# Where the low halves of the weights are formed, and how far ahead

## The chip, the cores and the metric

One core of a Trainium2 chip runs the whole program. The metric is device time in microseconds (us), from one launch. Engines: TensorE (PE, with its weight loads PEld), VectorE (DVE), ScalarE (ACT), GpSimd (POOL) and SyncE (SP), which issues the loads.

## The reference

Two transformer blocks in float32, on 512 tokens of 1024 features. What matters here:

```python
# first block: h = rms_norm(x)
proj = h @ w_in                      # r, k, v, decay, rate, gate, memory query
def step(S, inp):                    # delta rule, 12 heads of 64
    sa = einsum(S, a_t)
    S = S * w_t + sa * b_t + v_t * k_t
    return S, einsum(S, r_t)
x = x + concat([mix, mem_out]) @ w_out
x = x + square(relu(rms_norm(x) @ w_ff1)) @ w_ff2
# second block: two attentions, each with its gate
y = sigmoid(g_a) * (o_a @ w_branch_a) + sigmoid(g_b) * (o_b @ w_branch_b)
x = x + y @ w_out
x = x + (silu(h @ w_gate) * (h @ w_up)) @ w_down
```

## The kernel before

**Products with weights.** Every large product is made of three matmuls per block of 128 x 128: high half of the weights by high half of the activations, low by high, high by low. `weight_block` (L1083) issues them. The weights come as 216 units of 128 x 1024 float32 (`unit_list`, L2593), loaded by SP (`load`, L2509). The ScalarE function `split` (L2081) waits for the load and for the last matmul of the unit that used the same buffers before, and copies `Wraw` to `Whi` at the lower precision (L2090). Then `Wlo = Wraw - Whi` is formed: by DVE (L1643) if the plan gave the unit the kind "wlo", by POOL (L2418) if it gave "wlo_pool". PE's first block of a tile waits for this subtraction. There are three sets of buffers in turn (`NW = 3`); units 3 and 29 have sets of their own. A load waits for the subtraction that last read its `Wraw`.

**The plan.** `make_plan` (L197) writes one list of steps by hand-made rules, and each engine runs its own steps of that list in this order; it never goes past a step that waits. The helper `unit` (L230) is called when a tile starts on a new unit `u` and first puts into the list the splits of all units up to `u + ahead - 1` (`splits`, L220), so that with `ahead` 2 the split of unit `u + 1` stands in front of tile `u`. The state `lo` says which engine gets the subtraction.

```python
    def unit(name):
        u = state["units"]
        state["units"] += 1
        splits(u + state["ahead"])
        return u
```

**Stages in order of time.** First projections; then the recurrence over six head pairs, where `blend` (L173) mixes the steps of one pair's block inverse (`inverse`, L514: scores "xm" and "sb", turned copies "na", then five levels of "t1", "xt" and "xu", the last one "yu") with the projections of the next pair (`ahead`, L488) and the state steps and the tail of the pair before (`states`, L542, `tail`, L558). A pair consumes three units (key, receptance, value), so it holds three splits. In the plan they stand as follows:

- slot A: behind the first level's "xu", a state step and the key tile's shift; next come "t1" and "xt" of level 2, a state step, the scan of the decays ("cum", DVE L1791), "xu", a state step, and the exponentials (ACT)
- slot B: behind the third level's "xu" and the next tile's shift; next come "t1" and "xt" of level 4, the group norm's root (reciprocal and the copy that widens it, DVE L1677 and L1680), "kk" and "xu"
- slot C: behind the value tile's shift, "xm" (DVE L1829) and the bonus (DVE L1812); next comes "sb", seven masked copies on DVE (L1829, L1855, into MT, Yi and BR), whose banks PE needs for "na"

DVE's part of "t1" is L1879 (T), of "xu" L1886 (Xi), of a state step L1915 (PD), of "yu" L1893. POOL has in the recurrence some small steps of its own, as the addition of the identity to Xi and Yi (L2479). In the last pair the first tiles of the output product take the filler's place; the splits of units 28 and 29 stand together between two state steps.

Then the first block's output product and feed-forward stage, the second block's projections, its two attentions with gate tiles and branch tiles between them (`weave`, L164), the joined branches (kind "both": 4 units "bb", each for two tiles of four blocks; `evict`, L1747: multiply by the gate, add the other branch (L1754), cast on ACT (L2171), subtract (L1756)), and the second output product and feed-forward stage.

`ahead` is 2 from the start of the recurrence (L611) to the end, apart from one tile. `lo` is "wlo_pool" in the recurrence (set L613, reset L636) and from the attentions to the end of the joined branches (set L716, reset L742): 17 units (13 to 29) and 24 units (117 to 140).

Of the kernel before, what the change touches and what calls it, by code (L numbers as in the profile page):

```python
# [25 lines left out]
NW = 3  # L26
# [34 lines left out]
class Plan:  # L61
# [9 lines left out]
    def step(self, kind, *key):  # L71
        self.steps.append((kind, *key))
        self.count(kind, *key)
# [55 lines left out]
def run(gen):  # L129
    for _ in gen:  # L130
        pass


def turns(*gens):
    gens = list(gens)
    while gens:
        for g in list(gens):
            try:
                yield next(g)
            except StopIteration:  # L140
                gens.remove(g)
# [50 lines left out]
def spaced(gen, took):  # L192
    for _ in gen:
        yield took


def make_plan(units):  # L197
# [9 lines left out]
    state = {"loads": 0, "splits": 0, "units": 0, "lo": "wlo", "ahead": 1, "held": None}  # L207
    pend = []

    def flush():  # L210
        now, pend[:] = pend[:], []
        for f in now:
            f()
# [222 lines left out]
    def mem_attention():  # L436

        def item(n):
            hp, j = divmod(n, 4)
            for i in range(2):  # L440
                M.take(("ms", n, i))
            step("ms", n)
            for i in range(2):
                M.give(("ms", n, i))
            yield 0.4
            step("mn", n)
            yield from rounds(SOFT_ROUNDS)
            bank("mt", n)
            yield 0.5
            if j == 0:  # L450
                M.take(("mpv", hp))
            step("mv", n)
            if j == 3:
                step("mpv", hp)
                step("mpv_lo", hp)
                M.give(("mpv", hp))
            yield 0.5
        yield from pipeline([item(n) for n in range(8)])
# [24 lines left out]
    def bonus(p):  # L483
        step("bo", p)
        ftmp.give(("sq", p))
        yield 1.0
# [55 lines left out]
    def states(p, room=0.2):  # L542

        two("uw", p)
        yield 1.0
        two("pd", p)
        yield 0.5
        two("phi", p)
        yield 0.6
        two("yo1", p)  # L550
        yield 0.6
        for ch in range(1, NC - 1):
            step("st", p, ch)
            yield room
        bank("yo2", p)
        yield 0.9

    def tail(p):  # L558
        step("gsq", p)
        yield 0  # L560
        bank("root", "t", p)
        yield 0.9
        yield 0
        bank("tn", p)
        yield 0.5
        yield 0
        bank("tg", p)
        yield 1.0
        step("tlo", p)
        count("Ulo", "mix", p)  # L570
        yield 0
# [38 lines left out]
    flush()  # L610
    state["ahead"] = NW - 1  # L611

    state["lo"] = "wlo_pool"  # L613
    mem_att = mem_attention()
    mix_order = (0, 1, 2, 3, 4, 6, 7, 5)
    for p in range(NP - 1):
# [7 lines left out]
    def beside():  # L624
        yield from turns(itertools.chain(bonus(NP - 1), states(NP - 2), tail(NP - 2)), mem_att)
        step("Xload")
        for i, g in enumerate(outs):

            state["ahead"] = (NW - 1, NW, NW - 1)[i]
            yield from spaced(itertools.islice(g, 7), 0.8)  # L630
        state["ahead"] = NW - 1

    filler = beside()
    blend(itertools.chain(inverse(NP - 1), states(NP - 1, 0.6), spaced(tail(NP - 1), 1)), filler, FILL_LAST)
    run(filler)
# [99 lines left out]
    flush()  # L735
    flush()

    for m in range(4):
        hold = []
        run(tile("both", (2 * m,), ("bb", m), "att", range(4, 8), hold=hold, last=False))  # L740
        run(tile("both", (2 * m + 1,), ("bb", m), "att", range(4, 8), j0=4, keep=hold[0]))
    state["lo"] = "wlo"  # L742
    for i in range(8):
        run(tile("res", ("gffn2", i), ("wo2", i), "y2", range(8)))
    ahead_of.append(norm(("n", "gffn2")))
# [57 lines left out]

def block_program(nc, xT, memT, wts, vecs, cst, w2a2, g2, biasA, biasB, xN, memN, out, units):
    plan = make_plan(units)
    N = lambda *key: plan.numbers[key]
    tiles = plan.tiles
# [1942 lines left out]
```

## Time and profile before

| | |
|---|---|
| three runs | 1519.39, 1523.72, 1524.26 us |
| median | 1523.72 us |
| profiled execution | 1518.95 us, its span 1517.2 us |
| busy in the span | PE 1462.2 (96%), PEld 1156.8 (76%), DVE 800.4 (53%), ACT 552.7 (36%), POOL 239.4 (16%) |
| mean granted TensorE clock | 0.997 of full speed |
| DMA | 130.89 MB, mean 86 GB/s |

The profile is one execution. Busy time is the sum of an engine's instructions; what matters for an engine in order is also where it stands still, and until what. In timeline rows the first number is the start in us from the span's start, the second the length, then engine, line, operation, output<-inputs, shapes and count; in square brackets the idle time before and what ended it.

### The profile page before, as it was taken

Reading aid. Unit: us, or ns where it says so; the run is one execution under the profiler, and the core shown is the slowest. Engines: PE = TensorE matmul, PEld = TensorE weight load, DVE = VectorE, ACT = ScalarE, POOL = GpSimd, SP = SyncE. Lnnn points to the kernel's source line nnn. Section 1 sums busy time; section 2 is a strip of 40 time slices with the busy share of each in tenths; the row PEclk is TensorE's granted clock in tenths of the full one; section 3 lists DMA queues with packets and bytes.
Section 4 is the critical chain, followed back from the end, with each engine's and each line's share of the span. In section 5 each row is a group of like instructions: output and inputs, shape, how many; then the busy total and the mean of one; then the engine's idle time right before and its main releaser. Section 6 shows DMA issues by size and latency. Waiting matters only on the chain.

```text
span 1517.2 us, 26650 instructions
## 1 busy us (share of the span) xinstructions
PE 1462.2 (96%) x11374; PEld 1156.8 (76%) x11374; DVE 800.4 (53%) x1261; ACT 552.7 (36%) x942; POOL 239.4 (16%) x166
## 2 busy tenths in 40 slices
PE   7999999979999999999999999999999999999999
PEld 6867777756788888888788766767777888888887
DVE  5655566664564444535644358577554443443343
ACT  7444434363422221312442256545333221222221
POOL 0233333201200000000110012222322210220120
PEclk9999999999999999999999999999999999999999
DMA  8311011011223232333233133311222333323223
GB/s 323 112 30 44 30 30 44 23 52 58 70 87 108 84 108 87 98 97 97 84 97 96 58 107 96 94 56 53 83 92 89 97 97 98 97 85 109 84 88 107
DMA packets 39334, 130.89 MB, mean 86 GB/s; under 512 B 4272, under 2 KB 5296, under 8 KB 39216
## 3 DMA queue, kind: packets, MB, share of 16 engines
q1 hardware_dynamic: 39216, 129.18, 26.9%
q8 instruction: 90, 1.47, 0.4%
q14 instruction: 28, 0.23, 0.0%
HBM read 127.07 MB, written 2.10 MB: 85 GB/s over the span
## 4 chain that ended last, share of the span: by engine, by line
PE 82%; DVE 8%; ACT 4%; issue 3%; POOL 0%; POOLq 0%; ACTq 0%; DVEq 0%
PE bank L1047 79%; PE bank L1447 1%; DVE Wlo L1643 1%; ACT Whi L2090 1%; DVE qa L1754 1%; DVE z L1680 0%; DVE Xi L1886 0%; DVE qa L1752 0%; ACT Hhi L2171 0%; PE bank L1161 0%; DVE X L1725 0%; ACT kbr L2337 0%; ACT slab L2306 0%; PE bank L1237 0%; ACT tmpb L2205 0%
## 5 line engine op out<-in xcount | busy, mean ns | idle before, releaser
L1047 PE MATMUL bank<-Hhi,Whi 128*128 128x512 f32 x912 | 375.8, 412 | 11.6 <-DVE Wlo L1643 8.4
L1047 PE MATMUL bank<-Hhi,Wlo 128*128 128x512 f32 x912 | 360.9, 396 | 0.0
L1047 PE MATMUL bank<-Hlo,Whi 128*128 128x512 f32 x912 | 357.6, 392 | 0.0
L1047 PE MATMUL bank<-Uhi,Whi 128*128 128x512 f32 x736 | 290.9, 395 | 8.1 <-POOL Wlo L2418 3.1
L1047 PE MATMUL bank<-Uhi,Wlo 128*128 128x512 f32 x736 | 287.2, 390 | 0.0
L1047 PE MATMUL bank<-Ulo,Whi 128*128 128x512 f32 x736 | 287.0, 390 | 0.0
L2090 ACT CAST Whi<-Wraw 128x1024 fp32r<-128x1024 f32 (+1 forms) x216 | 222.9, 1036 | 164.2 <-PE bank L1047 148.2
L1643 DVE TENSOR_TENSOR Wlo<-Wraw,Whi 128x1024 fp32r<-128x1024 f32 (+1 forms) x175 | 224.2, 1282 | 98.9 <-ACT Whi L2090 98.8
L1047 PEld LDWEIGHTS bank<-Hhi,Whi 128*128 128x128 f32 x912 | 171.5, 188 | 66.0 <-issue 12.3
L1047 PEld LDWEIGHTS bank<-Hlo,Whi 128*128 128x128 f32 x912 | 171.9, 188 | 42.1
L1047 PEld LDWEIGHTS bank<-Hhi,Wlo 128*128 128x128 f32 x912 | 172.0, 189 | 34.0 <-issue 1.2
L1047 PEld LDWEIGHTS bank<-Uhi,Whi 128*128 128x128 f32 x736 | 138.1, 188 | 45.2 <-DVE Wlo L1643 5.5
L1047 PEld LDWEIGHTS bank<-Ulo,Whi 128*128 128x128 f32 x736 | 138.3, 188 | 29.4
L1047 PEld LDWEIGHTS bank<-Uhi,Wlo 128*128 128x128 f32 x736 | 138.3, 188 | 27.8 <-issue 0.2
L2418 POOL TENSOR_TENSOR Wlo<-Wraw,Whi 128x1024 fp32r<-128x1024 f32 x41 | 99.8, 2433 | 367.1 <-ACT Whi L2090 366.4
L1725 DVE TENSOR_TENSOR X<-X,bank 128x512 f32<-128x512 f32 x72 | 49.5, 688 | 168.8 <-PE bank L1047 168.7
L2426 POOL TENSOR_TENSOR accb<-accb,tmpb 128x512 f32<-128x512 f32 x14 | 18.8, 1344 | 383.9 <-ACT tmpb L2205 383.9
L2165 ACT CAST Uhi<-tmpb 128x512 fp32r<-128x512 f32 x32 | 19.8, 619 | 148.0 <-DVE tmpb L1734 148.0
L2431 POOL TENSOR_TENSOR qa<-qa 128x512 f32<-128x512 f32 x22 | 28.5, 1295 | 198.9 <-ACT qa L2175 198.9
L2179 ACT CAST Hhi<-qa 128x512 fp32r<-128x512 f32 x22 | 13.7, 622 | 116.0 <-POOL qa L2436 116.0
L2347 ACT ACTIVATE sr<-sr,st 128x256 f32<-128x256 f32 (+1 forms) x64 | 33.7, 528 | 36.6 <-DVE st L2015 19.8
L1732 DVE SCALAR_TENSOR_TENSOR tmpb<-bank,RSb 128x512 f32<-128x512 f32 x32 | 22.1, 692 | 44.8 <-PE bank L1047 44.6
(292 smaller groups left out, 1571.8 us busy)
## 6 DMA issues: line engine op xcount, KB each, us to landing
Wraw<-in_wts SPq DMA_DIRECT2D x208, 512.0 KB, 3.5
bA<-in_biasA SPq DMA_DIRECT2D x12, 256.0 KB, 2.8
Wraw<-in_wts SPq DMA_DIRECT2D x8, 384.0 KB, 3.2
x<-in_xT SPq DMA_DIRECT2D x8, 256.0 KB, 4.4
x_rows<-in_xN SPq DMA_DIRECT2D x2, 1024.0 KB, 8.3
X<-in_xT SPq DMA_DIRECT2D x2, 1024.0 KB, 7.2
out<-X SPq DMA_DIRECT2D x8, 256.0 KB, 2.1
bB<-in_biasB SPq DMA_DIRECT2D x4, 384.0 KB, 3.1
```

The costliest lines, as they stand in the source:

```text
L1047: return e.matmul(o, lhsT, rhs, start=start, stop=stop, skip_group_check=True)
L1447: p = e.transpose(o, sr[n % 3][:, x:x + 128], c("ident"))
L1643: e.tensor_tensor(Wsp[k][1][:, 0:width], Wraw[k][:, 0:width], Wsp[k][0][:, 0:width].bitcast(F), ALU.subtract).then_inc(S["wlo"])
L1725: e.tensor_tensor(y, y, z, ALU.add).then_inc(S["evict"])
L1732: e.scalar_tensor_tensor(z[:], b[:], 0.0, RSb[:], ALU.max, ALU.mult).then_inc(S["evict"])
L1754: e.tensor_tensor(z[:], z[:], gates[i], ALU.add).then_inc(S["gated"])
L2090: e.copy(Wsp[k][0][:, 0:width], Wraw[k][:, 0:width]).then_inc(S["whi"])
L2165: e.copy(Uhi[:, x.key[1], :], tmp_of(("raw", t))[:]).then_inc(S["ffhi"])
L2347: p = e.activation(part, part, ACT.Exp, scale=1.0, bias=x[:, 2 + i:3 + i], accum_out=x[:, 4 + i:5 + i])
L2418: done(e.tensor_tensor(Wsp[k][1][:, 0:width], Wraw[k][:, 0:width], Wsp[k][0][:, 0:width].bitcast(F), ALU.subtract), "wlo_pool")
L2426: done(e.tensor_tensor(accb[:], accb[:], tmp_of(("sqr", *x.key))[:], ALU.add), "sq_add")
L2431: done(e.tensor_tensor(z[:], z[:], s[:], ALU.mult), "sig")
```

## The change

`lo` stays "wlo" (DVE) through the recurrence, `ahead` becomes 3 from the end of the recurrence on, where it was set back to 2, and `lo` goes back to "wlo" before the joined branches and not after them. Nothing else differs.

```diff
@@ -610,7 +610,6 @@
     flush()
     state["ahead"] = NW - 1
 
-    state["lo"] = "wlo_pool"
     mem_att = mem_attention()
     mix_order = (0, 1, 2, 3, 4, 6, 7, 5)
     for p in range(NP - 1):
@@ -628,7 +627,7 @@
 
             state["ahead"] = (NW - 1, NW, NW - 1)[i]
             yield from spaced(itertools.islice(g, 7), 0.8)
-        state["ahead"] = NW - 1
+        state["ahead"] = NW
 
     filler = beside()
     blend(itertools.chain(inverse(NP - 1), states(NP - 1, 0.6), spaced(tail(NP - 1), 1)), filler, FILL_LAST)
@@ -735,11 +734,11 @@
     flush()
     flush()
 
+    state["lo"] = "wlo"
     for m in range(4):
         hold = []
         run(tile("both", (2 * m,), ("bb", m), "att", range(4, 8), hold=hold, last=False))
         run(tile("both", (2 * m + 1,), ("bb", m), "att", range(4, 8), j0=4, keep=hold[0]))
-    state["lo"] = "wlo"
     for i in range(8):
         run(tile("res", ("gffn2", i), ("wo2", i), "y2", range(8)))
     ahead_of.append(norm(("n", "gffn2")))
```

## Rows read from the trace of the kernel before

**Rows 1.** The tile Wlo of the whole span: duration min/median/max in ns.
```profile
L1643 DVE TENSOR_TENSOR Wlo<-Wraw,Whi x175: 951/1226/1652, 6.7 to 1506.3; 128x1024 fp32r<-128x1024 f32 x167, 128x768 fp32r<-128x768 f32 x8
L2418 POOL TENSOR_TENSOR Wlo<-Wraw,Whi x41: 2347/2385/2932, 88.1 to 1099.9; 128x1024 fp32r<-128x1024 f32 x41
```

**Rows 2.** Busy time by stage: PE, PEld, DVE, ACT, POOL (x instructions), clock, DMA, GB/s.
```profile
85.00:385.00 300.00, 271.97 (x5655) 209.01 (x5652) 179.20 (x400) 127.33 (x270) 83.48 (x60) 0.99 0.13 39
1075.00:1110.00 35.00, 29.83 (x127) 23.30 (x127) 25.33 (x28) 11.23 (x16) 9.46 (x4) 1.00 0.25 77
```

**Rows 3.** Timeline of 179 to 184, slot A of one head pair.
```profile
179.62 0.76 DVE L1879 TENSOR_TENSOR T<-bank,C 128x256 f32<-128x256 f32 x2 [0.53 <-PE bank L1047]
179.81 1.03 ACT L2090 CAST Whi<-Wraw 128x1024 fp32r<-128x1024 f32 x1
180.48 1.21 DVE L1791 TENSOR_TENSOR_SCAN sg<-C,sg 128x512 f32<-128x512 f32 x1
180.93 2.93 POOL L2418 TENSOR_TENSOR Wlo<-Wraw,Whi 128x1024 fp32r<-128x1024 f32 x1 [2.38 <-ACT Whi L2090]
181.65 0.69 PE L1047 MATMUL bank<-T,Yi 64*64 64x64 f32 x32
183.09 0.27 DVE L1915 SCALAR_TENSOR_TENSOR PD<-bank,PC,PD 128x64 f32<-128x64 f32 x1
183.47 0.33 PE L1047 MATMUL bank<-PD,AR 64*64 64x64 f32 x4
```

**Rows 4.** Timelines of 185 to 199, slot B of the same pair.
```profile
185.96 0.43 DVE L1680 COPY ftmp<-st 128x512 f32<-128x512 f32 x1
192.87 1.03 ACT L2090 CAST Whi<-Wraw 128x1024 fp32r<-128x1024 f32 x1
194.57 0.69 PE L1047 MATMUL bank<-T,Yi 64*64 64x64 f32 x32
194.97 1.67 DVE L1680 COPY z<-st 128x512 f32<-128x512 f32 x1
197.22 0.74 DVE L1886 TENSOR_TENSOR Xi<-bank,Xi 128x256 f32<-128x256 f32 x2
198.02 0.69 PE L1047 MATMUL bank<-Xi,MT 64*64 64x64 f32 x32 [0.67 <-DVE Xi L1886]
```

**Rows 5.** Timeline of 207 to 212, slot C of the same pair.
```profile
207.72 0.68 DVE L1812 SCALAR_TENSOR_TENSOR bonus<-bank,slab 128x512 f32<-128x512 f32 x1
207.89 1.29 POOL L2479 TENSOR_TENSOR Xi<-Xi,C 128x512 f32<-128x512 f32 x1 [3.94 <-DVE Xi L1829]
211.03 0.69 PE L1047 MATMUL bank<-C,AR 64*64 64x64 f32 x32 [1.79 <-DVE BR L1829]
```

**Rows 6.** Timeline of 101 to 104: a DVE operation beside one of POOL.
```profile
101.64 1.29 POOL L2470 TENSOR_TENSOR ta<-ta,kn 128x512 f32<-128x512 f32 x1
101.92 1.55 DVE L1820 TENSOR_TENSOR AR<-kn,Pp 128x512 f32<-128x512 f32 x1
```

**Rows 7.** Timeline of 368, the chain of state steps in the last head pair.
```profile
368.00 0.28 DVE L1915 SCALAR_TENSOR_TENSOR PD<-bank,PC,PD 128x64 f32<-128x64 f32 x1 [0.87 <-PE bank L1047]
```

**Rows 8.** Timelines of four places late in the kernel.
```profile
741.02 0.19 PEld L1047 LDWEIGHTS bank<-Uhi,Whi 128*128 128x128 f32 x1 [0.55 <-DVE Wlo L1643]
897.61 0.19 PEld L1047 LDWEIGHTS bank<-Hhi,Whi 128*128 128x128 f32 x1 [1.91 <-POOL Wlo L2418]
1092.85 2.56 DVE L1754 TENSOR_TENSOR qa<-qa,tmpb 128x512 f32<-128x512 f32 x1
1094.92 0.50 PE L1047 MATMUL bank<-Uhi,Whi 128*128 128x512 f32 x1 [1.68 <-POOL Wlo L2418]
```

**Rows 9.** A stretch at the lower clock, and POOL's slot A of the next two pairs.
```profile
260.00:264.00 4.00, 4.00 (x37) 3.30 (x29) 0.00 (x0) 0.91 (x3) 1.57 (x2) 0.59 0.42 131
229.51 2.92 POOL L2418 TENSOR_TENSOR Wlo<-Wraw,Whi 128x1024 fp32r<-128x1024 f32 x1 [2.39 <-ACT Whi L2090]
279.70 2.92 POOL L2418 TENSOR_TENSOR Wlo<-Wraw,Whi 128x1024 fp32r<-128x1024 f32 x1 [2.40 <-ACT Whi L2090]
```

## The prediction

> All times are microseconds unless ns is said. "Wlo" is the subtraction that forms the low half of a weight unit, "cast" the one on ScalarE that forms its high half. Units carry numbers 0 to 215 in the order of their use.
>
> **What bounds the kernel.** I read the engine totals first: TensorE (PE) is busy 96% of the span, DVE 53%, ACT 36%, POOL 16%. So a change of the other engines can pay or cost only through stalls of PE. The stage table says where stalls are: in the recurrence, 85 to 385, PE stands for 28 of 300, and over the joined branches (kind "both") for 5.2 of 35 [rows 2]; in the feed-forward stages it hardly stands. The list of waits and the timelines then name the releaser of each stall. In the recurrence PE never waits for a POOL Wlo: it waits for DVE results of the recurrence. Late in the kernel it does wait for Wlo of both engines [rows 8].
>
> **Part 1: Wlo of the recurrence moves from POOL to DVE.** Counting through the planner, POOL has units 13 to 29 there: 17 of the 41 in [rows 1]. POOL takes 2.39 for one, DVE 1.23 [rows 1]. The sum 17 x 1.23 = 21 isn't the price; it depends on what stands behind the Wlo in DVE's fixed order. The plan puts one at each of three places of a head pair.
>
> Slot A (units 16, 19, 22, 25; the planner's order is shift, cast, Wlo, then T of level 2, a state step, the scan). The cast ends at 180.84, so DVE, which has run T at 179.62 meanwhile, would stand until 180.9, run Wlo to 182.1 and T to 182.9. PE starts its matmuls on T at 181.65 without a wait now [rows 3]: it would start at 182.9, 1.3 late. Behind T stand a state step (0.3) and the 1.21 scan, so the addition to Xi (0.75) and the next state step (0.28, now at 183.09) end near 185.4, and PE, which needs that at 183.47, is 2.0 late altogether [rows 3]. ACT's exponentials wait for the same scan and come 2.7 later, with ScalarE's square root and DVE's reciprocal behind them; PE reaches the product that needs them with a little room. Four times 2.0 is 8.0. The first pair (unit 13) has no state steps, there only T counts: 1.4. Bounds: 1.2 each if only the subtraction counts, 2.8 if the late square root shows too. I take **9.4** (6 to 14).
>
> Slot B (units 14, 17, 20, 23, 26). The cast ends at 193.90, Wlo would run to 195.2 and T to 195.95, where PE has started on it at 194.57: 1.4 late [rows 4]. But the copy into z took 1.67 because POOL's Wlo ran beside it; the same form takes 0.43 without POOL (185.96), so I give 1.25 back [rows 4]. With it the addition to Xi, which waits for PE too, starts where it does now (197.22), and of PE's present wait of 0.67 the delay is hidden [rows 4]. What is left is 1.4 - 0.67 = 0.75, five times less a little in the first pair, whose T of the last level is late already: **3.5** (2 to 7).
>
> Slot C (units 15, 18, 21, 24). The cast is early. Wlo would stand between the bonus, which ends at 208.40, and seven masks of scores for whose last one PE already waits 1.79 [rows 5]. So its 1.25 adds in full. It also meets POOL's addition to Xi, which runs from 207.89 to 209.18 [rows 5]. What that does is seen elsewhere: a DVE product of two SBUF tensors that began at 101.92 beside POOL's 1.29 took 1.55 instead of about 0.7 [rows 5, 6]. It ran its own length once POOL was done, so Wlo would start near 209.2: 0.75 more. Four times 2.0: **8.0** (5 to 8).
>
> By the Trainium skill, "SBUF — State Buffer", section "Who interferes with whom", a DVE instruction with two SBUF inputs and a GpSimd one that reads SBUF exclude each other for the whole instruction. This trace agrees: 1.55 in [rows 6], 2.56 in [rows 8]. The rule speaks for this change at B and in the joined branches, and against it at C.
>
> Units 27 to 29, in the last pair. Unit 27 stands before the addition to Yi, behind which PE's solve waits; it costs between nothing and 1.23, and as slots A and B say that the cast comes late, I take 1.0. Units 28 and 29 stand together inside the chain of state steps, where DVE idles 0.87 per step [rows 7]; their casts are early, 2 x 1.23 less that slack and a part of what DVE idles before: 1.2 (0.7 to 2.5). Together **2.2** (0.7 to 3.7).
>
> What POOL gains is worth nothing: its steps of the recurrence wait for ACT, PE or DVE, and the 2.9 of its Wlo in slot A is over before the exponentials are done in the new order.
>
> Sum of part 1: 9.4 + 3.5 + 8.0 + 2.2 = 23.1.
>
> **The clock.** In one of four equal slots C the TensorE clock fell: between 260 and 264 the granted share was 0.59, thus 1.2 GHz for most of it against 2.4 around [rows 9], after a stall like the 1.79 of [rows 5]. That pair took 279.70 - 229.51 = 50.19, the one before it 229.51 - 180.93 = 48.58 [rows 3, 9]: 1.6 for one fall. The stall at C would be near 3.8 now, so more of them should be followed by a fall. I take two more, **3.2** (0 to 10).
>
> **Part 2: look-ahead of three units.** From unit 29 on, each split stands one tile earlier. On ACT the cast of unit u+2 now waits for the last matmul of unit u-1, but it stands behind the eviction of that tile, which waits for the same; on DVE and on SP's queue (a load waits for the Wlo of three units before) the order is the same with the index shifted. So no wait is added except for one extra split at unit 29, behind which PE has a tile to run (24 matmuls, by 29.83 for 127 of them 5.6 [rows 2]). What goes are PE's waits for Wlo from unit 31 on: six before the second block's norm, the longer ones 0.55 of weight load [rows 8], of which part is hidden under the matmul before, 1.1 in all; 1.5 of the 1.91 at the start of the attention [rows 8]; an estimated 0.8 in small ones later. The wait for unit 30's Wlo stays, since its split stands where it stood. Sum: -3.4 (0 to -6).
>
> **Part 3: Wlo of the joined branches on DVE.** POOL's Wlo blocks a DVE addition there, 2.56 for about 0.7, and PE waits 1.68 for the Wlo itself [rows 8]. DVE wins 1.9 a unit and pays 1.23, and the Wlo is no longer urgent. But the chain of evictions on DVE (multiply, add, wait for ACT's cast, subtract, twice per unit) is longer than PE's 5.6 per unit, and PE has two banks: it stays a bit late. Of PE's 5.2 [rows 2] I take half back: **-2.7** (+1 to -5.2). POOL keeps 20 Wlo (units 118 to 137), all in the attention, at an unchanged price.
>
> **Sum.** 23.1 + 3.2 - 3.4 - 2.7 = +20.2 on the profiled execution's 1518.95 gives 1539.2. The runs shown are 1519.39, 1523.72 and 1524.26, so the profiled one lies 4.8 under their median, and by the median I would get 1543.9. I put the forecast between: **1541**.
>
> **Rivals.**
> 1. *Faster.* Each Wlo runs in an idle stretch of DVE, and PE's later waits swallow the delays. For it: DVE is busy only 179 of 300 [rows 2]. It decides if the casts end well before DVE comes to the Wlo. Then all that is left are parts 2 and 3, -6.1 and at most -11: 1513 to 1518. Against it: in slots A and B the cast ends 1.2 and 0.8 after DVE wanted to go on. Chance 0.10.
> 2. *No change.* A third of the slots cost, the others are covered: about +6 - 6, 1519 to 1524. Chance 0.08.
> 3. *The clock falls at every A and C.* About eight more falls of 1.6, thus +13 where I took 3: 1550 to 1556. Chance 0.18. The Trainium skill, "TensorE: Matmul & The Clock Gate", section "What's actually happening", says that the clock is throttled by default and activity releases it; by that, a longer stall asks for a fall, and one of four here agrees so far [rows 9].
> 4. *The look-ahead does nothing*, since the cast that it moves waits for a tile that ends later; or the freed DVE time in the joined branches is lost to the chain there. Then 6 less is won: 1545 to 1550. Chance 0.12.
>
> The forecast's own case, 1530 to 1546, has 0.52. The range, 1527 to 1555, leaves out the faster rivals and the tail above. What a measurement of this kernel can tell from no change is 0.3%, about 4.6. Faster 0.10, same 0.08, slower 0.82.
>
> **What would show it.** Right: DVE with 196 Wlo and POOL with 20; the period of a head pair up from 48.6 to about 53; PE waiting about 1.3 for T in slot A and 3 to 4 for BR in slot C; DVE's Wlo in slot C near 2.0 long; the copy to z at 0.43; from 400 on a stage that is 5 to 7 shorter, with no waits like those of [rows 8]. Wrong: a pair period under 50 (the covers hold), or PE's waits of part 2 still there (the look-ahead doesn't reach), or a clock of 1.2 GHz in most pairs (the third rival).

## The result, and the profile after

| | before | after |
|---|---|---|
| median (lowest to highest) | 1523.16 us (1519.39 to 1524.26), 4 runs | 1541.35 us (1539.76 to 1544.11), 4 runs |
| ratio after / before | | 1.0128, 95% interval 1.0115 to 1.0141 |
| profiled execution, span | 1518.95, 1517.2 us | 1544.11, 1542.3 us |
| mean granted TensorE clock | 0.997 | 0.989 |

The change makes the kernel 18.2 us slower by the medians (+1.2%; the ratio in the table, which is not simply that of the two medians, gives +1.28%, or 19.5 us). The two profiled executions lie 25.2 apart, since the one of before was the fastest of its runs and the one of after the slowest of its own. Offsets below are between these two, for the same DVE operation in both traces; they add up to 25, not to 18.

The engine totals of the page and two of its groups of instructions after the change, line by line with busy time, mean ns of one, and the idle time before with its releaser:

```profile
PE 1472.4 (95%) x11374; PEld 1167.0 (76%) x11374; DVE 814.6 (53%) x1282; ACT 553.3 (36%) x942; POOL 187.2 (12%) x145
L1642 DVE TENSOR_TENSOR Wlo<-Wraw,Whi 128x1024 fp32r<-128x1024 f32 (+1 forms) x196 | 252.8, 1291 | 139.7 <-ACT Whi L2089 139.6
L2417 POOL TENSOR_TENSOR Wlo<-Wraw,Whi 128x1024 fp32r<-128x1024 f32 x20 | 47.8, 2391 | 253.6 <-ACT Whi L2089 253.6
```

The instructions moved as the plan says: 196 on DVE and 20 on POOL, against 175 and 41 in [rows 1]. The totals say nothing of the 25 us: PE is busy 10 us longer (the same number of matmuls, more of them at the lower clock), DVE is at 53% as before. The offsets by stage do:

| up to (us in after's trace) | offset | step |
|---|---|---|
| 85, start of the recurrence | 0 within 0.9 | 0 |
| 398, its end | +29.4 | +29 |
| 770, end of the first feed-forward stage | +27.8 | -1.6 |
| 1104, start of the joined branches | +29.1 | +1.3 |
| 1141, their end | +26.9 | -2.1 |
| 1516, last feed-forward stage | +25.2 | -1.8 |

So all of the loss is in the recurrence, and the later stages give 4 back, less than the 7.2 by which the same stages are shorter with parts 2 and 3 alone (below). What makes PE stand in the recurrence, from the list of PE's waits over 85 to 405 (in total, times, longest):

```profile
PE bank L1046 <- DVE BR L1828: 14.8, 5, 3.7
PE bank L1046 <- DVE T L1878: 7.8, 6, 2.5
PE bank L1160 <- DVE T L1878: 5.4, 4, 1.4
```

and the same list of the kernel before, over 85 to 385:

```profile
PE bank L1047 <- DVE BR L1829: 7.2, 4, 1.8
PE bank L1047 <- DVE T L1879: 0.7, 1, 0.7
```

None of these rows names a Wlo. Three sources of stalls are new or doubled, and they are the three places of a head pair at which a subtraction was put on DVE. The timeline shows each; here slot A, which answers to [rows 3]:

```profile
193.72 1.23 DVE L1642 TENSOR_TENSOR Wlo<-Wraw,Whi 128x1024 fp32r<-128x1024 f32 x1 [1.79 <-ACT Whi L2089]
194.86 0.75 DVE L1878 TENSOR_TENSOR T<-bank,C 128x256 f32<-128x256 f32 x2
195.76 0.69 PE L1046 MATMUL bank<-T,Yi 64*64 64x64 f32 x32 [1.20 <-DVE T L1878]
197.83 0.33 PE L1046 MATMUL bank<-PD,AR 64*64 64x64 f32 x4 [0.18 <-DVE PD L1914]
200.44 0.17 DVE L1670 TENSOR_SCALAR st<-st 128x8 f32<-128x8 f32 x1 [2.66 <-ACT st L2130]
```

DVE stands 1.79 until the cast is there, works 1.23, and only then comes to T. PE, which had no wait here, has one of 1.20. Slot B, which answers to [rows 4]:

```profile
208.42 1.22 DVE L1642 TENSOR_TENSOR Wlo<-Wraw,Whi 128x1024 fp32r<-128x1024 f32 x1 [0.70 <-ACT Whi L2089]
210.04 0.66 PE L1160 MATMUL bank<-C,ftmp 128*128 128x128 f32 x4 [1.35 <-DVE T L1878]
210.46 0.43 DVE L1679 COPY z<-st 128x512 f32<-128x512 f32 x1
213.27 0.69 PE L1046 MATMUL bank<-Xi,MT 64*64 64x64 f32 x32
```

PE waits 1.35 for T and has lost the wait of 0.67 on Xi; the copy into z takes 0.43 instead of 1.67. Slot C, which answers to [rows 5]:

```profile
223.13 1.28 POOL L2478 TENSOR_TENSOR Xi<-Xi,C 128x512 f32<-128x512 f32 x1 [3.69 <-DVE Xi L1828]
223.57 1.92 DVE L1642 TENSOR_TENSOR Wlo<-Wraw,Whi 128x1024 fp32r<-128x1024 f32 x1
228.00 0.69 PE L1046 MATMUL bank<-C,AR 64*64 64x64 f32 x32 [3.51 <-DVE BR L1828]
229.21 0.63 PE L1046 MATMUL bank<-Hhi,Wlo 128*128 128x512 f32 x1
```

The subtraction takes 1.92 here and not 1.23: it gets almost nothing done until POOL's addition ends at 224.41, and needs 1.08 from there. PE waits 3.51 where it waited 1.79. The last row is the second part of the price: directly behind the stall a matmul that takes 0.40 elsewhere takes 0.63. The windows give the granted clock of that stretch (last but two of the columns), as in [rows 9]:

```profile
228.00:232.00 4.00, 4.00 (x42) 3.25 (x43) 0.18 (x1) 0.65 (x2) 0.74 (x1) 0.58 0.11 46
```

0.58 granted is 1.2 GHz for most of the 4 us, against 2.4 around. Before, one of the four slots C was followed by such a fall (at 261), and one more comes in the last pair, at 308. After, all four slots C have one (at 119, 174, 229 and 283), three more come in the last pair, at 358, 375 and 399, and one in the first pair, at 92, behind its slot A: eight in the recurrence instead of two. At that last place PE stood 1.04 before and stands 2.49 now:

```profile
91.01 0.69 PE L1046 MATMUL bank<-T,Yi 64*64 64x64 f32 x32 [2.49 <-DVE T L1878]
```

The period of a pair is read off a copy that POOL makes once in each:

```profile
183.22 0.61 POOL L2495 COPY AR<-C 128x512 f32<-128x512 f32 x1 [8.70 <-PE bank L1046]
237.47 0.61 POOL L2495 COPY AR<-C 128x512 f32<-128x512 f32 x1 [8.73 <-PE bank L1046]
```

54.25, against 48.58 of a pair without a fall before [rows 3, 9]. Following the offset through the pair, these 5.67 are 1.65 at A, 0.76 at B, 1.73 at C and 1.54 behind the fall of the clock.

Late in the kernel, rows that answer to [rows 8] and the second of [rows 2], from the timelines and the windows:

```profile
421.43 0.19 PEld L1046 LDWEIGHTS bank<-Uhi,Whi 128*128 128x128 f32 x1 [2.25 <-DVE Wlo L1642]
927.26 0.70 PE L1046 MATMUL bank<-ka,qa 64*128 64x256 f32 x4 [2.15 <-DVE sr L2001]
1122.55 0.69 DVE L1753 TENSOR_TENSOR qa<-qa,tmpb 128x512 f32<-128x512 f32 x1
1122.66 0.47 PE L1046 MATMUL bank<-Uhi,Whi 128*128 128x512 f32 x1 [1.28 <-DVE qa L1751]
1103.00:1138.00 35.00, 31.94 (x137) 24.98 (x136) 23.63 (x32) 11.51 (x16) 0.50 (x1) 1.00 0.25 80
```

The wait for unit 30 stays, as its split did. The waits of 0.55 before the second block's norm are gone, and so is the one for Wlo at the start of the attention. But PE now stands 2.15 at the next dependence there, on a chain that has nothing to do with weights, where the timeline of the kernel before has

```profile
899.43 0.70 PE L1047 MATMUL bank<-ka,qa 64*128 64x256 f32 x4 [0.42 <-DVE sr L2002]
```

so nothing was won at that place, and the clock falls behind the longer stall. In the joined branches the addition takes 0.69 instead of 2.56 and PE no longer waits for a Wlo at that place; it waits 1.28 for the multiplication ahead of it. PE stands 3.1 of 35 us there, where it stood 5.2.

### The profile page after: what moved, and what is told of

It reads as the page before. It is cut to its first block, busy times and chain, and to the rows that moved or that the text cites. A ratio compares the mean times of both kernels' runs of the same rounds, so it can differ in the third digit from the quotient of the medians.

```text
span 1542.3 us, 26630 instructions
## 1 busy us (share of the span) xinstructions
PE 1472.4 (95%) x11374; PEld 1167.0 (76%) x11374; DVE 814.6 (53%) x1282; ACT 553.3 (36%) x942; POOL 187.2 (12%) x145
## 4 chain that ended last, share of the span: by engine, by line
PE 80%; DVE 8%; ACT 4%; issue 3%; POOLq 0%; POOL 0%; ACTq 0%; DVEq 0%
PE bank L1046 78%; DVE Wlo L1642 1%; PE bank L1446 1%; ACT Whi L2089 1%; PE bank L1160 1%; DVE slab L1773 0%; DVE qa L1753 0%; DVE qa L1751 0%; DVE T L1878 0%; DVE Yi L1854 0%; DVE ftmp L1699 0%; PE bank L1236 0%; ACT kbr L2336 0%; DVE sg L1790 0%; DVE MT L1828 0%
## 5 line engine op out<-in xcount | busy, mean ns | idle before, releaser
L1642 DVE TENSOR_TENSOR Wlo<-Wraw,Whi 128x1024 fp32r<-128x1024 f32 (+1 forms) x196 | 252.8, 1291 | 139.7 <-ACT Whi L2089 139.6
L1046 PEld LDWEIGHTS bank<-Ulo,Whi 128*128 128x128 f32 x736 | 138.4, 188 | 29.4
L2417 POOL TENSOR_TENSOR Wlo<-Wraw,Whi 128x1024 fp32r<-128x1024 f32 x20 | 47.8, 2391 | 253.6 <-ACT Whi L2089 253.6
```

The lines of the kernel that those rows point to most:

```text
L1046: return e.matmul(o, lhsT, rhs, start=start, stop=stop, skip_group_check=True)
L1642: e.tensor_tensor(Wsp[k][1][:, 0:width], Wraw[k][:, 0:width], Wsp[k][0][:, 0:width].bitcast(F), ALU.subtract).then_inc(S["wlo"])
L2417: done(e.tensor_tensor(Wsp[k][1][:, 0:width], Wraw[k][:, 0:width], Wsp[k][0][:, 0:width].bitcast(F), ALU.subtract), "wlo_pool")
```

## The experiments

Twelve kernels. "Before" in each group is the median of the kernel before on the same chip in the same series.

### The three parts of the change by themselves

Part 1 alone (the change without its other two edits):

```diff
-        state["ahead"] = NW
+        state["ahead"] = NW - 1
...
-    state["lo"] = "wlo"
     for m in range(4):
...
+    state["lo"] = "wlo"
```

> Part 1 alone: the 17 subtractions of the recurrence on DVE, the rest as before. Theory (the place in DVE's order is the price, and the clock falls after the longer stalls): the head pair goes from 48.6 to 54.3 as in the changed kernel, the time by 24 to 29 us over the kernel before, so more than the whole change costs, since parts 2 and 3 give 4 back. Rival (the look-ahead or the joined branches carry a part of the loss): less than the whole change, under +18.

Part 2 alone, part 3 alone, and both, each on the kernel before:

```diff
-        state["ahead"] = NW - 1
+        state["ahead"] = NW
```

> Part 2 alone: look-ahead of three units after the recurrence. Theory: the waits at 735 to 769 and the small ones after 1166 go, the stall at the start of the attention only changes its releaser, and in the joined branches POOL's subtraction is no longer waited for but DVE's chain, slowed by the blocked additions, is: -2 to -4 us. Rival (the casts that now wait for a later tile hold ACT up in the attention): 0 to +3, with the attention stage longer by more than 2.

```diff
+    state["lo"] = "wlo"
     for m in range(4):
...
-    state["lo"] = "wlo"
```

> Part 3 alone: four subtractions around the joined branches on DVE, look-ahead two. Theory (the DVE chain of 2 x 2.8 and 1.2 is the bound there, 7.0 per unit against 7.4): -1.5 to -3 us, with additions of 0.69 and not 2.56. Rival (with look-ahead two PE waits for the subtraction itself behind the chain, and the unit stays at 7.4 or more): 0 to -0.5.

> Parts 2 and 3 without part 1: the recurrence as before. Theory: all of the loss is part 1, so this is 4 to 5 us faster than the kernel before, 1518 to 1520. Rival (the parts need each other, as part 1 also freed POOL): no faster than before.

| kernel | median us | difference | ratio to before (1521.43), 95% |
|---|---|---|---|
| part 1 | 1546.93 | +25.5 | 1.0167 (1.0153 to 1.0181) |
| part 2 | 1519.49 | -1.9 | 0.9987 (0.9978 to 0.9996) |
| part 3 | 1520.57 | -0.9 | 0.9991 (0.9982 to 1.0000) |
| parts 2 and 3 | 1514.83 | -6.6 | 0.9956 (0.9944 to 0.9969) |

Part 1 costs 25, and nothing else costs anything: its trace is 29.9 behind that of before at the end of the recurrence and 29.5 behind at the end. Part 2's gain is just under the 2 that was its lower bound and part 3's under its 1.5, with an interval that reaches to no change; and by the medians the two parts gain more together than the 2.8 of both alone; the intervals overlap, though (at most 6.1 for the sum, at least 4.7 for both), so that isn't shown. Both together missed their own forecast of 4 to 5 on the good side. The offsets against before, stage by stage behind the recurrence, say where:

| | first feed-forward stage | attention | joined branches | later |
|---|---|---|---|---|
| part 2 | -1.6 | -1.7 | +1.2 | -1.8 |
| part 3 | 0 | +0.1 | -1.6 | -0.3 |
| parts 2 and 3 | -1.6 | -1.7 | -2.1 | -1.8 |
| the whole change | -1.6 | +1.3 | -2.1 | -1.8 |

The -1.6 and the -1.8 are the look-ahead's, the same in each kernel that has it. The attention column is the clock but for 0.3: the kernel before falls to 1.2 GHz at 1018, with part 2 alone and with parts 2 and 3 that fall doesn't come, and the whole change has it (at 1047, which is the same place) and another one at 927. The +1.2 of part 2 has a fall in it too (at 1106). Part 3 repairs the blocked addition, as its timeline shows against the 2.56 of [rows 8]:

```profile
1096.01 0.69 DVE L1754 TENSOR_TENSOR qa<-qa,tmpb 128x512 f32<-128x512 f32 x1
```

So without the falls part 2 is worth 3.4 and part 3 about 2, and both together 5.5: they simply add. What decides on those falls was not isolated.

### The three slots by themselves

On the kernel before, one set of units goes to DVE and the rest stays on POOL:

```diff
-            plan.numbers[("lo", u)] = state["lo"]
+            lo = "wlo" if u in (13, 16, 19, 22, 25) else state["lo"]
+            plan.numbers[("lo", u)] = lo
             step("split", u)
-            count(state["lo"], u)
+            count(lo, u)
```

> The kernel before with only the five subtractions of slot A on DVE. Theory (each slot has its own price, read from the changed kernel's trace: 1.65 per pair, 1.3 in the first): +7 to +9 us, PE waiting 1.2 for T, few new falls of the clock. Rival (the price is DVE's total load, 17 subtractions alike): 5 of 17 of part 1, so +7.5 as well, but then slot B costs as much as slot A.

The same with the units (14, 17, 20, 23, 26):

> Only the five of slot B on DVE. Theory: 0.76 per pair, since the copy into z is freed from POOL and PE's later wait of 0.67 is used up: +3 to +4.5 us. Rival (equal prices): +7.5.

And with (15, 18, 21, 24):

> Only the four of slot C on DVE. Theory: 1.73 of later start per pair and 1.55 for a fall of the clock after each stall of 3.5, less the one or two falls that the kernel before has anyway: +10 to +13 us, with four falls just behind the stalls. Rival (equal prices): 4 of 17, +6. Second rival (the falls come whatever the stall's length): +7, with no more falls than before.

| slot | median us | difference | ratio to before (1522.50), 95% |
|---|---|---|---|
| A, 5 units | 1532.34 | +9.8 | 1.0064 (1.0045 to 1.0084) |
| B, 5 units | 1523.52 | +1.0 by medians, +2.0 by the ratio | 1.0013 (1.0000 to 1.0026) |
| C, 4 units | 1536.64 | +14.1 by medians, +13.4 by the ratio | 1.0088 (1.0070 to 1.0106) |

By the ratios the same instruction costs 1.9 at A, 0.4 at B and 3.4 at C, per unit. That each move costs its own 1.23 is refuted, and so is a common price for the three. By the ratios the three sum to 9.7 + 2.0 + 13.4 = 25.1 of part 1's 25.4. Each interval is 2 to 3 us to either side, so this says that the slots are most of it, and not that units 27 to 29, which were not moved alone, cost nothing. The forecasts were missed by a little at all three: A and C cost more than their upper bounds of 9 and 13, and their traces have more time at the lower clock than was counted on; B cost less than its 3.

The pair period splits each into delay and clock. Slot A alone, three pairs in a row, the same POOL copy:

```profile
176.95 0.61 POOL L2497 COPY AR<-C 128x512 f32<-128x512 f32 x1 [7.46 <-PE bank L1048]
...
228.73 0.61 POOL L2497 COPY AR<-C 128x512 f32<-128x512 f32 x1 [7.44 <-PE bank L1048]
...
278.95 0.61 POOL L2497 COPY AR<-C 128x512 f32<-128x512 f32 x1 [5.84 <-PE bank L1048]
```

The pair between 228.73 and 278.95 takes 50.22, thus 1.64 more than 48.58, and has no fall of the clock; the one from 176.95 to 228.73 takes 51.78 and has one, at 220. The fall is 1.56. Slot B alone:

```profile
171.98 0.61 POOL L2497 COPY AR<-C 128x512 f32<-128x512 f32 x1 [5.87 <-PE bank L1048]
221.36 0.61 POOL L2497 COPY AR<-C 128x512 f32<-128x512 f32 x1 [5.86 <-PE bank L1048]
```

49.38, thus 0.80 more, without a fall. Slot C alone, the copy of three pairs, and windows around two of the stalls:

```profile
179.34 0.61 POOL L2497 COPY AR<-C 128x512 f32<-128x512 f32 x1 [8.74 <-PE bank L1048]
...
231.14 0.61 POOL L2497 COPY AR<-C 128x512 f32<-128x512 f32 x1 [8.69 <-PE bank L1048]
...
284.29 0.61 POOL L2497 COPY AR<-C 128x512 f32<-128x512 f32 x1 [10.03 <-PE bank L1048]
...
118.00:124.00 6.00, 6.00 (x75) 5.19 (x74) 0.00 (x0) 1.84 (x4) 0.00 (x0) 0.60 0.00 0
169.00:175.00 6.00, 5.15 (x54) 4.31 (x54) 1.00 (x3) 1.25 (x3) 1.27 (x1) 0.72 0.17 67
```

The granted share is 0.60 and 0.72, and the clock falls at the stalls at C of the other two pairs as well (falls at 116, 171, 222 and 273). The first and the last of the four low stretches are twice as long as the others. PE's list of waits has 14.2 for BR in four stalls, so 3.5 each. The pair takes 231.14 - 179.34 = 51.80, 3.2 more: 1.7 for the delay and 1.5 for the clock. The next one, with the long fall, takes 284.29 - 231.14 = 53.15, so that fall cost some 2.9. In this profiled execution two such falls add 2.7 to what slot C costs in the changed kernel's. The moved operation delays PE once, and the stall that it makes longer then slows PE again.

### Is it the stall, or the operation? PE gets work for it

If the price lies in PE standing idle, then it goes away when PE has something else to do there, with every subtraction where the change put it. On the changed kernel, two matmul steps that stood behind the copies "na" of a pair are moved ahead of them, so that PE runs them while DVE is still at the masks:

```diff
     assert state["units"] == len(units)
+    for p in range(1, NP - 1):
+        at = plan.steps.index(("na", p))
+        for _ in range(2):
+            i = next(i for i in range(at, len(plan.steps)) if plan.steps[i][0] == "mm")
+            plan.steps.insert(at, plan.steps.pop(i))
+            at += 1
```

> The changed kernel, with PE's next two blocks of the weight tile moved ahead of the turned copy that stalls in slot C (pairs 1 to 4). Theory (the stall of 3.5 is what makes the clock fall): the stall shrinks to 2.1 and most of the falls behind it go, so 1.4 + 1.5 per pair, -8 to -12 us against the changed kernel. Rival (falls don't depend on it): -5 to -6. Second rival (what follows the turned copy is late instead, as ScalarE's copies and the next products wait for it): 0 to -2.

1529.48 us, ratio to before 1.0041 (1.0027 to 1.0055): 11.9 less than the changed kernel by the medians of two series, 13.2 by the ratios. Its timeline at slot C, and the pair period:

```profile
217.88 1.93 DVE L1648 TENSOR_TENSOR Wlo<-Wraw,Whi 128x1024 fp32r<-128x1024 f32 x1
222.32 0.69 PE L1052 MATMUL bank<-C,AR 64*64 64x64 f32 x32 [1.91 <-DVE BR L1834]
...
177.51 0.61 POOL L2501 COPY AR<-C 128x512 f32<-128x512 f32 x1 [5.74 <-PE bank L1052]
228.79 0.61 POOL L2501 COPY AR<-C 128x512 f32<-128x512 f32 x1 [5.72 <-PE bank L1052]
```

DVE's operation still takes 1.93, but PE waits 1.91 and not 3.51, the period is 51.28 and not 54.25, and of the four falls behind slot C none is left. 1.6 of the 2.97 is the shorter stall, and the other 1.4 about what a fall costs.

### The same operations on DVE, placed where DVE has time

The opposite test leaves the amount of work on DVE and takes it out of the way. DVE's subtraction of unit 13 + 3p, 14 + 3p and 15 + 3p becomes a step of its own. It stands later in DVE's order only: before the next pair's square root (A), before the last step "yu" of the inverse (B), and behind the masks of the scores (C). Units 27 to 29 get places of their own too, and every other unit keeps the place it had.

```diff
     assert state["units"] == len(units)
+    late_lo = {}
+    for p in range(NP - 1):
+        late_lo[13 + 3 * p], late_lo[14 + 3 * p] = ("root", "f", p + 1), ("yu", p)
+        if p < NP - 2:
+            late_lo[15 + 3 * p] = ("uw", p)
+    late_lo[27], late_lo[28], late_lo[29] = ("uw", 5), ("gsq", 5), ("tn", 5)
+    for u in range(len(units)):
+        at = plan.steps.index(("split", u)) + 1
+        if u in late_lo:
+            at = plan.steps.index(late_lo[u], at)
+        plan.steps.insert(at, ("low", u))
...
-        steps = {"split": split, "x": token,
+        steps = {"low": split, "x": token,
```

The last two lines are DVE's table of steps. The move of the experiment above isn't in it.

> The changed kernel with all 17 subtractions of the recurrence still on DVE, but each later in DVE's order, at a place where DVE stands idle in the trace: slot A ahead of the reciprocal of the keys' norm, slot B ahead of the addition to Yi, slot C behind the masks, those of the last pair behind the addition to Yi, the last state output and the group norm's copy. Theory (the place is the price, not the load): part 1 costs at most 1 us, or gains up to 3, since POOL no longer blocks the copy into z: 1511 to 1516, 26 to 30 under the changed kernel. Rival (DVE's added 21 us of work show wherever they stand): at least 10 us of part 1's loss stay, over 1524.

1511.38 us, ratio 0.9933 (0.9915 to 0.9951): 30 less than the changed kernel, and faster than before. From its timelines:

```profile
170.74 0.61 POOL L2506 COPY AR<-C 128x512 f32<-128x512 f32 x1 [7.16 <-PE bank L1057]
195.32 0.43 DVE L1690 COPY z<-st 128x512 f32<-128x512 f32 x1
202.25 1.22 DVE L1653 TENSOR_TENSOR Wlo<-Wraw,Whi 128x1024 fp32r<-128x1024 f32 x1
202.47 2.13 POOL L2486 TENSOR_TENSOR kf<-kf,Pi 128x512 f32<-128x512 f32 x1 [4.71 <-DVE ftmp L1815]
218.49 0.61 POOL L2506 COPY AR<-C 128x512 f32<-128x512 f32 x1 [7.17 <-PE bank L1057]
```

The period is 47.75, below the 48.58 of before. The 17 subtractions take DVE 23.4 us here and 23.6 in the changed kernel, and they cost the kernel's time nothing. It even comes out under the kernel with parts 2 and 3 alone (0.9956, 1514.83), which still has POOL's subtractions in the recurrence. The intervals of the two ratios overlap, but the periods show the gain: the copy into z is at 0.43 in each pair instead of 1.67, and the pair is 0.83 shorter. So what was moved wasn't the price; what it was put in front of was.

Both edits together, on the changed kernel:

> The one before, and two blocks of the weight tile ahead of the turned copy in slot C, whose stall is 1.8 there. Theory: 1.4 per pair and the falls of the clock behind it: 5 to 8 us under the one before. Rival (what follows the turned copy is late instead): 0 to -2.

1503.79 us (1501.71 to 1505.67), ratio 0.9888 (0.9863 to 0.9912). Slot C there, and the period:

```profile
207.09 0.69 PE L1063 MATMUL bank<-C,AR 64*64 64x64 f32 x32 [0.19 <-DVE BR L1845]
207.19 1.74 DVE L1659 TENSOR_TENSOR Wlo<-Wraw,Whi 128x1024 fp32r<-128x1024 f32 x1
...
167.23 0.61 POOL L2512 COPY AR<-C 128x512 f32<-128x512 f32 x1 [5.72 <-PE bank L1063]
213.56 0.61 POOL L2512 COPY AR<-C 128x512 f32<-128x512 f32 x1 [5.72 <-PE bank L1063]
```

PE's wait is 0.19 (0.5 in the first pair), the subtraction starts once the masks are done, where its 1.74 (still beside POOL) hinders nobody, and the period is 46.33. The profiled execution, 1502.09, has one stretch at 1.2 GHz, at 323, and a mean granted clock of 0.999. Of the four executions two are like it (1501.71 and 1502.09); the other two have 0.995 and took 1505.50 and 1505.67, so the falls come back in some executions of this kernel too. It computes all that the kernel before does and is 17.2 faster than it, about 37 faster than the changed one: the best version found here.

### How much of that is the move of matmuls alone

Two controls with the same move as above, one on the kernel before, one on the kernel with parts 2 and 3 (Wlo of the recurrence on POOL in both):

> The kernel before with only the move of two blocks of the weight tile ahead of the turned copy. Theory (the stall of 1.8 in slot C is there without the change and fillable): 1.4 per pair in four pairs, and the falls of the clock behind it: 5 to 8 us faster than the kernel before. Rival (it pays only where the subtraction stands in slot C): 0 to -2.

> The same move with parts 2 and 3, and the recurrence's subtractions on POOL: the best order with POOL, to set beside the one with the subtractions late on DVE. Theory (POOL's only price is the blocked copy in slot B, 0.7 to 0.8 per pair): 3 to 4 us slower than that one, so 1506 to 1509. Rival (POOL and the late places on DVE are worth the same): 1502 to 1505.

| kernel | median us | ratio to its before, 95% | pair period |
|---|---|---|---|
| before, move | 1513.98 | 0.9951 (0.9935 to 0.9968) | 47.14 |
| parts 2 and 3, move | 1508.50 | 0.9919 (0.9904 to 0.9933) | 47.14 |
| the change, subtractions late, move | 1503.79 | 0.9888 (0.9863 to 0.9912) | 46.33 |

The move is worth 7.5 on the kernel before, parts 2 and 3 another 5.5 and the subtractions on DVE, at good places, a last 4.7, which was measured across two series and whose intervals just overlap. The traces say the same: the periods are 47.14 - 46.33 = 0.81 apart in three pairs and 0.48 in the first, and the last pair has that copy too; together some 3.7 if that copy is worth 0.8 there too. As the copy into z is what differs there, 0.43 for 1.67, I put it down to that again. So DVE is the better engine for these subtractions, if they stand in the right places.

## Why the prediction was right

The forecast was 1541, measured were 1541.35 (ratio 1.0128, 1.0115 to 1.0141); the likeliest case held, slower, between 1530 and 1546. It was worked out as +20.2 on the profiled execution; the medians differ by 18.2, the profiled executions by 25.2. The mechanism of each slot held. That the number came within 0.4 us is luck. In the traces the delays of part 1 are 2.6 less than forecast, the clock costs 5.8 more and parts 2 and 3 give 1.9 less, which makes 25.2. The medians lie nearer to the forecast since the two profiled executions are extreme in their falls. The profiled one of before has three falls and a mean granted clock of 0.997, where 36 of the 49 executions of that kernel in the series of the experiments have 0.994 to 0.996. The profiled one of after has ten and 0.989, where its other three have 0.991 and 0.992. That is 0.0011 for a fall. By an estimate from these figures, an ordinary pair of executions differs by about four falls and not by seven, some 5 us less. The base too was a choice, halfway between 1539.2 and 1543.9. By its steps:

- **What bounds the kernel.** Held: the loss is PE's stalls on DVE's results and the clock behind them, and the busy shares said nothing of it.
- **Slot A, 9.4.** The first wait is as forecast, 1.20 for 1.3. Alone it measured 9.7, but 1.65 a pair is delay (8 in all) and the rest is falls of the clock. The 2.0 was a bit too much, because I put DVE's operations end to end, while in the rows the next one starts before the last has ended: T at 194.86, where Wlo runs to 194.95. That is 0.08 each, over four operations. In the first pair the 1.4 for T is there too (the stall went from 1.04 to 2.49), but the fall of the clock behind it was not in the term.
- **Slot B, 3.5.** 0.76 a pair in the changed kernel, 0.80 alone, forecast 0.75. Both halves of it are in the rows: T late by 1.35, and the copy into z at 0.43. As a kernel of its own it measured 2.0 (0 to 4.0), which the 3.5 is inside of.
- **Slot C, 8.0.** 1.73 a pair, forecast 2.0. The exclusion by POOL was there: 1.92 for a 1.23 operation. By the Trainium skill, "SBUF — State Buffer", section "Who interferes with whom", a DVE instruction with two SBUF inputs and a GpSimd one that reads SBUF exclude each other; the rows of C agree, though the loss was 0.69 of POOL's 1.28 only, as POOL had begun 0.44 earlier. The prediction used that rule at B as well, where it doesn't say anything: the copy into z has one input. That it is blocked all the same is what the rows show, 1.67 beside POOL and 0.43 without. And the blocked operation doesn't run its whole own length once POOL is done, as the prediction read in [rows 6]: it ran 0.54 of about 0.7 from there, and the subtraction at C 1.08 of 1.23.
- **Units 27 to 29, 2.2.** Not measured alone. What is left of the 29 lost in the recurrence, after 8 + 4 + 7 for the slots and some 9 for the clock, is about 1.5.
- **The clock, 3.2: the term that was mis-sized.** In the two traces the recurrence has eight falls against two, and the six more cost about 9 (1.55 each, some of the last pair less). I had the mechanism, and in one pair of the kernel before its price (1.6, measured 1.54 to 1.56), but guessed how often: "more of them should be followed by a fall. I take two more". With a stall of 3.5 it was every slot C, in the changed kernel and again with slot C alone. The third rival was half true: every C, but slot A of a steady pair never by its own stall of 1.2. The prediction's own sign of being wrong in this, "a clock of 1.2 GHz in most pairs", is there, and with six more falls the traces lie nearer to that rival's eight than to the two of the forecast. The delays came out smaller than forecast (about 20.5 for 23.1), so part of the error was covered.
- **Part 2, -3.4, and part 3, -2.7.** Together they measured -6.6 by themselves, against a sum of -6.1; in the changed kernel only 4.2 came back by the offsets. The look-ahead was worth its 3.4, but not where I put it: 1.6 before the second block's norm (1.1), nothing at the start of the attention (1.5), where a wait on DVE's chain took the place of the one on Wlo, and 1.8 later (0.8). The joined branches gave 2.1 (2.7). What is missing is the 1.3 of the fall of the clock at 927. The fourth rival has this much of the truth: where the wait for a weight went at the attention, another stood right behind it.
- **The first two rivals** are refuted. No slot was covered, the cheapest cost 0.76 a pair. But the experiments show under what condition the first would be true: with the subtractions elsewhere in DVE's order the very same change is 0.67% faster than before (0.9933, 0.9915 to 0.9951).

What stays open: why the fall at 927 comes in the changed kernel and not in the one with parts 2 and 3 alone, though both stall there alike (2.15 and 2.23). Of the seven kernels with look-ahead three, which all stall 2.2 at that place, three have the fall. And the terms above are for the profiled executions; how many falls an execution has can be told from its mean clock, but which ones can't be seen from one trace for each kernel.

## What to carry to other kernels

The price of an operation that is moved to an engine in order isn't its duration, nor does that engine's free share say it is free: it is what stands behind it there, and at three places of one loop the same 1.23 us cost 0.4, 1.9 and 3.4, the clock included. So move it to the engine *and* to a place in that engine's order behind the results that TensorE waits for; here that turned a loss of 18 into a gain of 10, of which 6.6 come from parts 2 and 3. Count a longer TensorE stall with the clock that falls behind it, and where a stall can't be shortened, give TensorE matmuls for it.

## What the runs showed of the hardware

- **The longer TensorE's stall, the more often the clock falls at it.** Stalls of 3.5 to 3.7 at slot C came with a stretch at 1.2 GHz in 12 of 12 cases (the changed kernel, part 1 alone, slot C alone), most of them worth 1.5 to 1.6 us, two of slot C alone twice as long and worth 2.9. Stalls of 2.5 in the first pair had one in 4 of 4 (the changed kernel with and without the move, part 1 alone, slot A alone), where the stall of 1.0 at the same place had none in 10 kernels. Stalls of 1.8 to 2.2 at slot C had one in 7 of 32: 1 of 4 each in the kernel before, with part 2, part 3, both, and the late subtractions, 2 of 4 with slot A alone, none of 4 with slot B alone and with the move on the changed kernel. With 0.2 to 0.5, in the three kernels with the move and no subtraction ahead of the masks, there was none in 12. In the middle it isn't the length that decides: of four equal stalls of 1.79 to 1.83, the fourth had the fall in the kernel before and the third with part 2, part 3 or both, where the recurrence is the same list of steps. By the Trainium skill, "TensorE: Matmul & The Clock Gate", section "What's actually happening", throttled is the default and activity releases it; the counts agree with that.
- **The exclusion between DVE and POOL runs both ways.** With the subtractions late, POOL's multiplication kf took 2.13 beside DVE's Wlo, where the same one takes 1.27 in the kernel before:

```profile
202.68 1.27 POOL L2476 TENSOR_TENSOR kf<-kf,Pi 128x512 f32<-128x512 f32 x1 [4.03 <-DVE ftmp L1805]
```

The pair's period was at its shortest without the move all the same, 47.75, so PE didn't pay for it.

- **Operations of DVE that follow each other without a wait overlap by about 0.08 us** as the trace shows them (the median of some 500 such pairs in each of the two traces; on ACT 0.09). That is nothing for one and 0.35 for a chain of four or five, the size of the error of slot A.
